# Gate and up products: the stream's high and low parts in one matmul of 512 columns

## What is computed

```python
def swiglu(h, w_gate, w_up, w_down):
    return (jax.nn.silu(h @ w_gate) * (h @ w_up)) @ w_down

h = rms_norm(x, g_ffn1_pre[l])
x = x + 0.5 * rms_norm(swiglu(h, w_ffn1_gate[l], w_ffn1_up[l], w_ffn1_down[l]), g_ffn1_post[l])
```

## Time and profile before

| what | value |
|---|---|
| median of 3 runs | 1420.91 us (1417.9 to 1424.04) |
| profiled execution, its own time | 1423.02 us |
| its span | 1420.9 us |
| mean granted clock of TensorE | 0.991 of full |
| TensorE matmul busy | 1377.3 us, 97% |
| TensorE weight load busy | 1233.6 us, 87% |
| VectorE busy | 1038.1 us, 73% |
| ScalarE busy | 748.8 us, 53% |
| gate and up stages, pairs 1 to 15 | about 40 to 347 us and 944 to 1254 us |

### The profile page before, as it was taken

One profiled execution on the slowest core, in us unless ns is written; L12 is line 12 of the kernel. 1 busy time (PEld: TensorE's weight loads), 2 busy tenths in 40 slices (PEclk: granted clock), 3 DMA queues, 4 the chain that ended last, 5 costly groups with the idle time before them and its releaser, 6 DMA issues.

```text
span 1420.9 us, 22721 instructions
## 1 busy us (share of the span) xinstructions
PE 1377.3 (97%) x8648; PEld 1233.6 (87%) x8648; DVE 1038.1 (73%) x1115; ACT 748.8 (53%) x1013; POOL 113.7 (8%) x164
## 2 busy tenths in 40 slices
PE   6999999999999999999999999989999999999997
PEld 6999999999788788767768888789999999987886
DVE  6977887788789964667664344687787778769896
ACT  5545544554685642667763333554544445457663
POOL 0000000001420000333220000000000000024100
PEclk9999999999999999999999999999999999999999
DMA  6233332337997654212113345232333233399974
GB/s 200 87 93 118 118 95 82 118 118 220 223 249 257 233 180 133 75 45 60 46 45 87 91 144 180 75 120 74 119 118 103 77 115 118 119 278 219 244 262 136
DMA packets 161638, 194.47 MB, mean 137 GB/s; under 512 B 6064, under 2 KB 116912, under 8 KB 161456
## 3 DMA queue, kind: packets, MB, share of 16 engines
q1 hardware_dynamic: 147808, 166.74, 36.4%
q0 software_dynamic: 13056, 25.17, 9.9%
q10 hardware_dynamic: 720, 1.84, 0.3%
HBM read 187.43 MB, written 6.29 MB: 136 GB/s over the span
## 4 chain that ended last, share of the span: by engine, by line
PE 80%; DVE 8%; DMA 6%; ACT 2%; issue 2%; POOL 1%; SPq 0%; DVEq 0%; ACTq 0%; POOLq 0%
PE ps L711 15%; PE ps L713 15%; PE ps L714 15%; PE ps L677 5%; PE ps L679 5%; PE ps L678 5%; PE ps L811 4%; PE ps L813 4%; PE ps L812 4%; DMA d_sum<-w_ffn_down 3%; DMA w_raw<-w_ffn_down 2%; PE ps L684 1%; PE ps L685 1%; PE ps L686 1%; PE ps L996 1%
## 5 line engine op out<-in xcount | busy, mean ns | idle before, releaser
L711 PE MATMUL ps<-s_hi,w_hi 128*128 128x256 f32 x960 | 273.2, 285 | 4.8 <-DVE w_lo L1655 4.8
L713 PE MATMUL ps<-s_lo,w_hi 128*128 128x256 f32 x960 | 272.9, 284 | 0.0
L714 PE MATMUL ps<-s_hi,w_lo 128*128 128x256 f32 x960 | 272.9, 284 | 0.0
L711 PE MATMUL ps<-a_hi,w_hi 128*128 128x256 f32 x816 | 233.1, 286 | 3.1 <-DVE a_lo L1610 3.0
L713 PE MATMUL ps<-a_lo,w_hi 128*128 128x256 f32 x816 | 232.7, 285 | 0.0
L714 PE MATMUL ps<-a_hi,w_lo 128*128 128x256 f32 x816 | 232.7, 285 | 0.0
L1184 ACT ACTIVATE w_hi<-w_sum 128x1024 fp32r<-128x1024 f32 x120 | 123.9, 1056 | 175.5 <-DVE w_sum L1682 80.4
L711 PEld LDWEIGHTS ps<-s_hi,w_hi 128*128 128x128 f32 x960 | 185.6, 193 | 5.1 <-DVE w_lo L1655 5.1
L713 PEld LDWEIGHTS ps<-s_lo,w_hi 128*128 128x128 f32 x960 | 185.7, 193 | 0.0
L714 PEld LDWEIGHTS ps<-s_hi,w_lo 128*128 128x128 f32 x960 | 185.6, 193 | 0.0
L811 PE MATMUL ps<-w_hi,l_hi 128*128 128x512 f32 x448 | 176.3, 394 | 8.7 <-DVE w_lo L1842 8.7
(11 more groups left out here) (205 smaller groups left out, 2553.2 us busy)
## 6 DMA issues: line engine op xcount, KB each, us to landing
w_raw<-w_ffn_down SPq DMA_DIRECT2D x72, 512.0 KB, 4.8
w_raw<-w_ffn_gate SPq DMA_DIRECT2D x64, 512.0 KB, 5.0
w_raw<-w_ffn_up SPq DMA_DIRECT2D x64, 512.0 KB, 4.8
d_sum<-w_ffn_down POOLq DMA_DIRECT2D x48, 512.0 KB, 8.7
w_raw<-w_in SPq DMA_DIRECT2D x44, 512.0 KB, 3.9
d_sum<-w_ffn_down SPq DMA_DIRECT2D x16, 512.0 KB, 11.8
d_m_raw<-w_ffn_down SPq DMA_DIRECT2D x8, 512.0 KB, 12.4
x_mid<-x_tok SPq DMA_DIRECT2D x8, 512.0 KB, 4.8
```

The source lines that it names most:

```text
L711: pe.matmul(o, wh, hi[:, k, :], start=first and f == 0 and k == 0, stop=False, skip_group_check=True)
L713: pe.matmul(o, wh, lo[:, k, :], start=False, stop=False, skip_group_check=True)
L714: mm = pe.matmul(o, wl, hi[:, k, :], start=False, stop=last and k == KH - 1, skip_group_check=True)
```

## The change

In products 2, 4 and 3 the stream's hi and lo parts, which now lie in one tile (`a1_both`, `a22_both`, `s4_both`), are the two halves of one moving operand of 512 columns for the weights' hi part. The third matmul (weights lo by stream hi) keeps 256 columns. So the low part's share ends in the second half of the bank and has to be added. For that every product has two banks, one for each f (sums in the first half, low shares in the second): `B_UP` takes four banks, `B_M2` and `B_DOWN` two each. `gate_first` and `gate_second` become two adds (`add_parts`), the second waiting for the first. For product 3, ScalarE copies the low share (`keep_low` into `m3_c`) and VectorE adds the sums (`up_first`) before `gated_first`. `summed` counts 6 a pair instead of 3, `copied` 4 instead of 3. In VectorE's queue `weights_lo(6)` moves from the start of the turn to the end of the turn before, between `sum_t4` and `sum_t1`. Products 1, 6, 7 and 5, pair 0 and the down stage keep their matmuls.

```diff
-        B_UP, B_M2, B_DOWN = (0, 1), 2, 3
+
+        B_UP, B_M2, B_DOWN = ((6, 7), (0, 1)), (4, 5), (2, 3)
...
+        def sums_of(banks):
+            return ps[:, banks[0]:banks[1] + 1, 0:HALF]
+
+        def low_of(banks):
+            return ps[:, banks[0]:banks[1] + 1, HALF:T]
...
-            def product_of(m, bank):
-                stream = {1: A11, 2: A12, 3: (s4_hi, s4_lo), 4: A22, 5: (s1_hi, s1_lo), 6: (s2_hi, s2_lo),
+            def product_of(m, banks):
+                hi, lo = {1: A11, 2: A12, 3: (s4_hi, s4_lo), 4: A22, 5: (s1_hi, s1_lo), 6: (s2_hi, s2_lo),
                           7: (s3_hi, s3_lo)}[m]
-                blocks(bank, (w_hi[PLACE[m]], w_lo[PLACE[m]]), *stream, m in (1, 2, 7), m in (2, 3, 4)
-                       ).then_inc(unit_done, 1)
+                both = {2: a1_both[:, :, KH:KD, :], 3: s4_both, 4: a22_both}.get(m)
+                for f in range(2):
+                    o = ps[:, banks[f], 0:HALF]
+                    for k in range(KH):
+                        col = (2 * k + f) * P
+                        wh, wl = w_hi[PLACE[m]][:, col:col + P], w_lo[PLACE[m]][:, col:col + P]
+                        first, last = m in (1, 2, 7) and k == 0, m in (2, 3, 4) and k == KH - 1
+                        if both is None:
+                            pe.matmul(o, wh, hi[:, k, :], start=first, stop=False, skip_group_check=True)
+                            pe.matmul(o, wh, lo[:, k, :], start=False, stop=False, skip_group_check=True)
+                        else:
+                            pe.matmul(ps[:, banks[f], :].rearrange("p (s t) -> p s t", s=2), wh, both[:, :, k, :],
+                                      start=first, stop=False, skip_group_check=True)
+                        mm = pe.matmul(o, wl, hi[:, k, :], start=False, stop=last, skip_group_check=True)
+                mm.then_inc(unit_done, 1)
...
-                    pe.wait_ge(a_done, b0 + 1)
+                    pe.wait_ge(comb_done, 8 * fi + 8)
                 else:
-                    pe.wait_ge(summed, p * 3 + (c0 - 2))
+                    pe.wait_ge(summed, p * SUMS + (c0 - 4))
                 product_of(2, B_M2)
                 pe.wait_ge(w_lo_done, p * PRODUCTS + (n0 + 4))
-                pe.wait_ge(copied, p * 3 + (c0 + 1))
+                pe.wait_ge(copied, p * COPIES + (k0 + 1))
                 if second:
                     pe.wait_ge(s_lo_done, 4 * fi + 1)
                 product_of(6, bank)
...
-                pe.wait_ge(summed, p * 3 + (c0 + 2))
+                pe.wait_ge(summed, p * SUMS + (c0 + 3))
...
-                        if m == 7:
+                        if m == 1:
+                            pe.wait_ge(summed, N_SUMS * (fi + 1) - 4)
+                            pe.wait_ge(a_done, NF * (fi + 1) - 2)
+                        elif m == 7:
                             pe.wait_ge(summed, N_SUMS * (fi + 1))
...
-                act_eng.activation(m1_c[:, :], ps[:, B_UP[par], :], ACT.Copy).then_inc(copied, 1)
+                act_eng.activation(pair_cols(m1_c), sums_of(B_UP[par]), ACT.Copy).then_inc(copied, 1)
...
+            def keep_low(fi, u0, p, par):
+                act_eng.wait_ge(unit_done, p * PRODUCTS + (u0 + PRODUCTS))
+                act_eng.wait_ge(a_done, p * 2 + NF * fi)
+                act_eng.activation(pair_cols(m3_c), low_of(B_UP[par]), ACT.Copy).then_inc(copied, 1)
 
...
-                    silu(p, p * 3 + (c0 + 3), True)
+                    silu(p, p * SUMS + (c0 + 5), True)
+                    keep_low(fi, u0, p, par)
...
-            def gate_first(u0, p, copies):
+            def add_parts(tile, banks, sums):
+                dve.tensor_tensor(pair_cols(tile), pair_cols(tile), sums_of(banks), ALU.add).then_inc(summed, 1)
+                dve.wait_ge(summed, sums + 1)
+                dve.tensor_tensor(pair_cols(tile), pair_cols(tile), low_of(banks), ALU.add).then_inc(summed, 1)
+            def gate_first(u0, p, copies, sums):
                 dve.wait_ge(copied, copies)
                 dve.wait_ge(unit_done, p * PRODUCTS + (u0 + PE_ORDER.index(2) + 1))
-                dve.tensor_tensor(m1_c[:, :], m1_c[:, :], ps[:, B_M2, :], ALU.add).then_inc(summed, 1)
+                add_parts(m1_c, B_M2, sums)
             def up_second(u0, p, par, copies):
                 dve.wait_ge(copied, copies)
                 dve.wait_ge(unit_done, p * PRODUCTS + (u0 + PE_ORDER.index(5) + 1))
-                dve.tensor_tensor(m7_c[:, :], m7_c[:, :], ps[:, B_UP[par], :], ALU.add).then_inc(summed, 1)
-
-            def gate_second(u0, p):
+                dve.tensor_tensor(pair_cols(m7_c), pair_cols(m7_c), sums_of(B_UP[par]), ALU.add).then_inc(summed, 1)
+            def gate_second(u0, p, sums):
                 dve.wait_ge(unit_done, p * PRODUCTS + (u0 + PE_ORDER.index(4) + 1))
-                dve.tensor_tensor(u2_c[:, :], u2_c[:, :], ps[:, B_DOWN, :], ALU.add).then_inc(summed, 1)
+                add_parts(u2_c, B_DOWN, sums)
             def gated_second(p, silus, sums):
                 a = act[:, :, 1, p, :]
                 dve.wait_ge(summed, sums)
                 dve.tensor_tensor(a, a, pair_cols(m7_c), ALU.mult).then_inc(a_done, 1)
-            def gated_first(u0, p, par, silus):
+            def up_first(p, par, copies):
+                dve.wait_ge(copied, copies)
+                dve.tensor_tensor(pair_cols(m3_c), pair_cols(m3_c), sums_of(B_UP[par]), ALU.add).then_inc(summed, 1)
+            def gated_first(p, silus, sums):
                 a = act[:, :, 0, p, :]
                 dve.wait_ge(silu_done, silus)
-                dve.wait_ge(unit_done, p * PRODUCTS + (u0 + PE_ORDER.index(3) + 1))
-                dve.tensor_tensor(a, a, bank_cols(B_UP[par]), ALU.mult).then_inc(a_done, 1)
+                dve.wait_ge(summed, sums)
+                dve.tensor_tensor(a, a, pair_cols(m3_c), ALU.mult).then_inc(a_done, 1)
...
-                    weights_lo(fi, u0, p, 6)
                     weights_lo(fi, u0, p, 5)
                     weights_lo(fi, u0, p, 4)
-                    gate_first(u0, p, p * 3 + (c0 + 1))
+                    gate_first(u0, p, p * COPIES + (k0 + 1), p * SUMS + c0)
...
-                    gate_second(u0, p)
+                    gate_second(u0, p, p * SUMS + (c0 + 3))
                     if last:
                         chunk_lo(fi, 1)
                     else:
                         weights_lo(fi, u0, p + 1, 7)
                         sum_t4(fi, u0, p + 1)
+                        weights_lo(fi, u0, p + 1, 6)
                         sum_t1(fi, u0, p + 1)
-                    gated_second(p, p * 2 + (s0 + 2), p * 3 + (c0 + 2))
-                    gated_first(u0, p, par, p * 2 + (s0 + 1))
+                    up_first(p, par, p * COPIES + (k0 + 4))
+                    gated_second(p, p * 2 + (s0 + 2), p * SUMS + (c0 + 3))
+                    gated_first(p, p * 2 + (s0 + 1), p * SUMS + (c0 + 6))
...
                 weights_lo(fi, u0, 1, 7)
                 sum_t4(fi, u0, 1)
+                weights_lo(fi, u0, 1, 6)
                 sum_t1(fi, u0, 1)
```

More of the change, by code:

```diff
@@ L239, in build @@
         act, ea = place("act", [P, 2, 2, NG, HALF], at=act_at)
[L240 to L244, removed]
+        a22_both, e = place("a22_both", [P, 2, KH, HALF], F32R, at=0)
+        a22_hi, a22_lo = a22_both[:, 0, :, :], a22_both[:, 1, :, :]
+        s4, _ = place("s4", [P, KH, HALF], at=e + KH * HALF * 4)
+        s4_both, e = place("s4_both", [P, 2, KH, HALF], F32R, at=e)
+        s4_hi, s4_lo = s4_both[:, 0, :, :], s4_both[:, 1, :, :]
         assert e == h_at
-        a1_hi, e = place("a1_hi", [P, KD, HALF], F32R, at=h_at)
-        a1_lo, e = place("a1_lo", [P, KD, HALF], F32R, at=e)
+        a1_both, e = place("a1_both", [P, 2, KD, HALF], F32R, at=h_at)
+        a1_hi, a1_lo = a1_both[:, 0, :, :], a1_both[:, 1, :, :]
         s1_hi, e = place("s1_hi", [P, KH, HALF], F32R, at=e)
@@ L258, in build @@
         a1, e1 = place("a1", [P, KD, HALF], at=e)
-        m7_c, _ = place("m7_c", [P, T], at=e)
+        m7_c, e3 = place("m7_c", [P, T], at=e)
+        m3_c, _ = place("m3_c", [P, T], at=e3)
         m1_c, e = place("m1_c", [P, T], at=e1)
@@ L477, in build @@
         T_ORDER = (7, 6, 4, 5)
-        N_SUMS = 3 * (NG - 1)
+        SUMS, COPIES = 6, 4
+        N_SUMS, N_COPIES = SUMS * (NG - 1), COPIES * (NG - 1)
         FIRST_AT = {RAW11: (w_hi[PLACE[1]], w_lo[PLACE[1]]), RAW21: (w_hi[PLACE[2]], w_lo[PLACE[2]]),
@@ L748, in pair @@
             def pair(fi, u0, p, par, second=False):
-                b0, c0, n0 = fi * NF, fi * N_SUMS - 3, u0
+                b0, c0, k0, n0 = fi * NF, fi * N_SUMS - SUMS, fi * N_COPIES - COPIES, u0
                 bank = B_UP[par]
@@ L771, in pair @@
                 else:
-                    pe.wait_ge(summed, p * 3 + c0)
+                    pe.wait_ge(summed, p * SUMS + (c0 - 1))
                 product_of(7, B_DOWN)
                 pe.wait_ge(w_lo_done, p * PRODUCTS + (n0 + 5))
-                pe.wait_ge(copied, p * 3 + (c0 + 2))
```

(24 more changed lines are left out.)

## The result

The changed kernel takes 1429.1 us (median of 7 runs, 1427.8 to 1432.7), the kernel before in the same rounds 1422.2. The ratio is 1.0067, 95% interval 1.0051 to 1.0083: slower, by 7 to 12 us. The profiled execution has a span of 1425.7 us, 4.8 more than that of before.

What follows compares the result with a forecast made beforehand. TensorE, 97% busy, bounded the kernel before; after, a latency loop through VectorE and ScalarE. Per FFN 1.25 + 2.8 + 1.15 is 5.2, 10.4 for both, plus 1.7 clock: +12.1 us on 1423.0, 1433 on the median, range 1418 to 1440.

Steps and rivals of the forecast that it cites:

- The direction and its cause: Before product 6, TensorE waits 0.46 us for keep_m1; the pair takes 20.37 us instead of 20.16, so the kernel slows.
- forecast steps: Times from the start of product 3 through VectorE's and ScalarE's queues, from the second add (0.92) to keep_m1 done (8.79).
- The price of a merge: In products 2, 4 and 3, each merged matmul saves 0.0133 us, 0.32 us a pair, if TensorE never waits.
- the faster rival: Before product 6, keep_m1 is early enough, so the merges' saving remains: 1412 to 1416 us; chance 0.10.
- Waits of VectorE for its own results: In VectorE's queue, an operation waiting for the one ahead starts later: 0.72 us for the second add, 1.26 for 1.13.
- Pair 1: In each FFN's first pair, the moved split makes sum_t1 and the already waiting product 6 1.25 us later, near 52.0.
- The clock: In the first FFN, idle time before product 6 of the first pair brings 1.2 GHz: +1.7 us, bounds 0 and 2.8.
- the one into the down stage: First w_down loads go out 1.65 us later, less 0.5 of room: +1.15 us for each FFN.
- the 28 loops: From product 6 of one pair to the next, fourteen loops in each FFN at 0.20 us: +2.8 us per FFN.

Runs made afterwards that it cites:

- a_split_late: The changed kernel with weights_lo(6) put back to the start of VectorE's turn, all added work kept: 1417.25 us, ratio 0.9974 to the kernel before.
- a_copy_first: The changed kernel with keep_m1 ahead of weights_hi 5 and 4 in ScalarE's turn, VectorE's queue untouched: 1413.2 us, ratio 0.9945 to the kernel before.
- a_up_early: The changed kernel with up_first moved one place ahead of sum_t1 in VectorE's turn, no instruction added: 1443.0 us, ratio 1.0149 to the kernel before.

## Why the prediction was right, and where it was off

- **The direction and its cause were right.** TensorE waits for `keep_m1` before product 6 in all 28 pairs from 2 on. Forecast 20.37 us a pair, measured 20.42; forecast steps 0.92, 1.53, 2.66, 3.92, 5.05, 6.30, 8.21, 8.79, measured 0.92, 1.53, 2.66, 3.91, 5.06, 6.31, 8.22, 8.80. a_split_late shortens the chain, a_copy_first takes it apart in another place, and both remove the wait; a_up_early lengthens it by 0.60 and the pair grows by 0.60.
- **The price of a merge was mis-sized**: 0.0133 us was the difference of the paces of each length alone; where matmuls of 512 and 256 columns alternate it is about 0.007 (0.17 us a pair over 24 merges; a product takes 2.82 for 2.77). In the loop that is 0.05 to 0.07 more in product 4, near enough the missing 0.05 of 20.42; the forecast of the faster rival (1412 to 1416) would have been too low by some 5 us for the same reason. The Trainium skill (TensorE: Matmul & The Clock Gate, Back-to-back issue gap) gives an isolated gap of N/2.4 ns plus about 2.5 ns, from which the estimate is 2.5 ns a merge; the 7 ns of the trace lie between that and the paces.
- **Waits of VectorE for its own results** cost 0.11 and 0.12 us again (146.05 to 146.77 for 0.61, 148.51 to 149.76 for 1.13). The Trainium skill says of its own measurement, eight copies, that the semaphore costs nothing extra (VectorE: DVE Perf Modes, The DRAIN you can't avoid); for these dependent neighbours the trace does not agree.
- **Pair 1**: `sum_t1` comes 1.33 us later against `sum_t3` (6.19 for 4.86 us in the first FFN), forecast 1.25. Product 6 of pair 1 started at 51.08 and not near 52.0, because this trace reached `sum_t3` 0.95 us earlier (41.06 for 42.01).
- **The clock**: forecast 1.7 us in the first FFN. Product 6 to product 4 took 10.19 us for 8.64, 1.55 lost, in the first trace. In the second nearly the same wait was followed by full clock. The first matmul of product 6 in the two traces, and a window of each behind the wait, columns as in the earlier trace rows (0.55 and 1.00 are the granted clock; 0.55 is 1.2 GHz that turns to 2.4 GHz within the window):

```profile
51.08 0.36 PE L745 MATMUL ps<-s_hi,w_hi 128*128 128x256 f32 x1 [2.49 <-DVE w_lo L1692]
...
53.00:55.00 2.00, 2.00 (x12) 2.00 (x12) 1.49 (x3) 1.58 (x2) 0.00 (x0) 0.55 0.94 296
```
```profile
51.17 0.35 PE L745 MATMUL ps<-s_hi,w_hi 128*128 128x256 f32 x1 [2.45 <-DVE w_lo L1692]
...
53.00:55.00 2.00, 2.00 (x19) 2.00 (x18) 1.49 (x3) 1.62 (x3) 0.00 (x0) 1.00 1.00 314
```

In the second FFN, where nothing was added for it, the clock cost 2.8 and 1.6 us in the two traces of before and 2.0 and 1.9 in those of after. On the means of both FFNs it cost the change some 0.5 us.

- **The term that failed is the one into the down stage**, +1.15 us for each FFN. The first loads did go out late, at 335.97 instead of 328.71, which is 1.8 us later than the down stage's own shift (352.91 against 347.43). But the landing that TensorE waits for did not move with them:

```profile
335.97 0.89 SPq L529 DMA_DIRECT2D w_raw<-w_ffn_down  x2
...
347.86 19.25 DMA d_sum<-w_ffn_down
```

It came at 367.11, 5.43 later than in the earlier trace rows, as much as the down stage: it goes by its own issue, at the end of product 5, and took 19.25 us for 19.41. Full DMA engines behind an early load did not mean that this load set the end. In the second FFN the sign is the other way: the waits in the down stage are 2.3 to 2.8 us shorter after, in both traces. Before, the load that this stage waits for last went out at 1253.10 and took 23.26 us; after, it went out at 1255.57 and took 19.38 us. What takes the second wait away was not tested. So the forecast of +12.1 stands against 6.4 us on the mean of two traces and 7 to 12 by the ratio: gate and up +10.4 (forecast 8.1 + 1.7), the rest -4.0 (forecast +2.3), of which the spread of the traces may be half. That gate and up came out so near its forecast is in part luck: the 28 loops cost 0.26 us each instead of 0.20, 1.7 more in all, and the clock 1.2 less.

## What to carry to other kernels

When an engine is at 97% and its helpers have a fifth of their time or more free, price an added operation by its place: write down, for each wait of the busy engine, the queue positions between the event that starts the chain and the one that ends it, and compare with the time that the busy engine takes to get there. Here 0.72 + 1.25 us in front of one sum turned 1.8 us of slack into a wait in each pair, and the copy, which needs nothing of what stood before it, gave it all back when it was moved two places up. A copy that only empties a buffer belongs in the queue where its own input is ready, not behind work that waits for somebody else.

## What the runs showed of the hardware

Matmuls of 512 and 256 columns that alternate take 0.353 us for one of each, where the paces of each length alone give 0.347. It makes no difference whether the 512 columns lie in one run or in two pieces (a pair of 19.98 to 19.99 us in both). A VectorE operation that waits for the result of the one ahead of it starts 0.11 to 0.12 us later than one that does not. A wait of 2.49 us on TensorE was followed by 1.2 GHz in one trace, and a wait of 2.45 us at the same place by 2.4 GHz in another of the same kernel.
